# Expert weights stored in blocks of 32 tokens instead of 16, the second block in four lent slots of the row ring

## The reference

```python
x = x + merged @ w_out                       # after pooling, attention and gates
h = rmsnorm(x, g_ffn)
q = (h @ w_query).reshape(C, 8, 2, 128)      # 8 heads, two halves
s = einsum('chpd,hpkd->chpk', q, sub_keys)   # 128 keys per half
sv, si = top_k(s, 16)                        # per half
cand = sv[:, :, 0, :, None] + sv[:, :, 1, None, :]
top_s, pos = top_k(cand, 16)                 # 16 of 256 sums, per head
idx = take_along_axis(cidx, pos)             # expert = 128 * i + j
gate = softmax(top_s)
hid = gelu(einsum('cd,chkd->chk', h, expert_u[idx])) * gate
x = x + einsum('chk,chkd->cd', hid, expert_v[idx])
y = rmsnorm(x, g_final)
```

## Time and profile before

| | us |
|---|---|
| runs | 2788.65, 2793.71, 2780.69; median 2788.65 |
| the profiled execution | 2784.83 |
| its span | 2783.0 |
| PE busy | 2589.6 (93%) |
| DVE busy | 2035.8 (73%) |
| POOL busy | 1556.3 (56%) |
| ACT busy | 537.8 (19%) |
| DMA | 996.18 MB, mean 358 GB/s |
| granted clock of TensorE, mean | 0.972 |

### The profile page before, as it was taken

The page is one execution under the profiler, slowest core; times in us unless marked ns, Lnnn a source line. Parts: engine busy times, 40 slices in busy tenths (PEclk is TensorE's granted clock), DMA queues, the critical chain, the costliest instruction groups (busy, mean ns, idle before and its releaser), DMA issues.

```text
span 2783.0 us, 30841 instructions
## 1 busy us (share of the span) xinstructions
PE 2589.6 (93%) x9957; PEld 1551.2 (56%) x9957; DVE 2035.8 (73%) x4558; ACT 537.8 (19%) x1206; POOL 1556.3 (56%) x1284
## 2 busy tenths in 40 slices
PE   7999989989997998998699999999999999999997
PEld 6867868875334475554554455455545455445553
DVE  1232977877348877788789988977777877877788
ACT  2141151211018014554510000100000000000101
POOL 0000155455665785444277786786777666766674
PEclk9999999989999999999799999999999999999998
DMA  6538789988997898999899999999999999999997
GB/s 239 184 120 299 282 310 406 405 320 312 395 374 254 324 411 319 336 350 333 296 362 413 413 412 413 391 408 413 413 412 413 413 413 413 415 412 413 413 404 285
DMA packets 305988, 996.18 MB, mean 358 GB/s; under 512 B 26432, under 2 KB 107200, under 8 KB 276672
## 3 DMA queue, kind: packets, MB, share of 16 engines
q0 software_dynamic: 184320, 671.17, 62.3%
q1 hardware_dynamic: 69664, 292.02, 26.9%
q10 hardware_dynamic: 51872, 31.46, 3.7%
HBM read 932.68 MB, written 61.87 MB: 357 GB/s over the span
## 4 chain that ended last, share of the span: by engine, by line
PE 34%; DMA 27%; DVE 19%; issue 12%; POOL 3%; ACT 3%; another core or an unknown queue 1%; DVEq 0%; ACTq 0%; POOLq 0%
PE bank L725 13%; DMA ring<-in_expert_v,idx 12%; PE bank L713 9%; DMA ring<-in_expert_u,idx 8%; DVE ring L1464 5%; DMA h<-in_expert_v,idx 3%; PE o_bank L745 3%; POOL ring L1429 2%; PE bank L784 2%; DVE region_b L1481 2%; PE bank L1011 2%; PE o_bank L1001 2%; DMA h<-in_expert_u,idx 1%; DMA region_c<-in_expert_u,idx 1%
## 5 line engine op out<-in xcount | busy, mean ns | idle before, releaser
L1429 POOL DMA_INDIRECT ring<-in_expert_u,idx x465 | 597.9, 1286 | 624.9 <-DVE idx L1772 292.6
L1011 PE MATMUL bank<-wslot,gate_attn 128*128 128x512 f32 x1536 | 690.0, 599 | 26.9 <-DVE gate_attn L1821 26.9
L1001 PE MATMUL o_bank<-region_a,wslot 128*128 128x384 f32 x2048 | 682.4, 487 | 0.0
L1429 POOL DMA_INDIRECT ring<-in_expert_v,idx x423 | 480.9, 1137 | 324.7 <-issue 134.6
L1001 PEld LDWEIGHTS o_bank<-region_a,wslot 128*128 128x128 f32 x2048 | 390.3, 191 | 297.9 <-issue 61.1
L1011 PEld LDWEIGHTS bank<-wslot,gate_attn 128*128 128x128 f32 x1536 | 293.4, 192 | 379.1 <-issue 314.3
L1464 DVE CUSTOM_DVE_ANT_0 ring<-ring,h 128x1024 f32<-128x1024 f32 x377 | 447.3, 1222 | 56.4 <-DMA ring<-in_expert_u,idx 48.6
L1481 DVE SCALAR_TENSOR_TENSOR region_b<-ring,dots,region_b 128x1024 f32<-128x1024 f32 x256 | 328.5, 1283 | 106.0 <-DMA ring<-in_expert_v,idx 78.5
L1331 ACT ACTIVATE gate_attn<-o_bank 128x384 f32<-128x384 f32 x128 | 62.7, 490 | 1241.8 <-PE o_bank L1001 1212.4
L725 PE MATMUL bank<-region_b,wslot 128*128 128x256 f32 (+1 forms) x768 | 232.3, 461 | 1.6 <-ACT region_b L1048 1.6
L725 PE MATMUL bank<-region_a,wslot 128*128 128x256 f32 (+1 forms) x768 | 226.3, 453 | 1.1 <-ACT region_a L1048 1.1
(11 more groups left out here) (214 smaller groups left out, 2860.7 us busy)
## 6 DMA issues: line engine op xcount, KB each, us to landing
wslot<-in_expert_uT SPq DMA_DIRECT2D x64, 1024.0 KB
wslot<-in_expert_v SPq DMA_DIRECT2D x64, 1024.0 KB
wslot<-kept_weights SPq DMA_DIRECT2D x53, 1024.0 KB
kept_weights<-wslot SPq DMA_DIRECT2D x29, 1024.0 KB, 8.6
expert_weights<-region_p ACTq DMA_DIRECT2D x24, 1024.0 KB
wslot<-in_w_in SPq DMA_DIRECT2D x13, 1024.0 KB
region_p<-expert_weights SPq DMA_DIRECT2D x8, 1536.0 KB
region_s<-expert_weights SPq DMA_DIRECT2D x7, 1536.0 KB
```

The lines of the kernel that those rows point to most:

```text
L1001: ins = nc.tensor.matmul(dense_in[q][:, 0:DENSE_T], u_cols[slot][:, k, :], mergeds[1][:, k, T - DENSE_T:T], start=(k == 0), stop=(k == KD ...
L1011: ins = nc.tensor.matmul(dense_out[2 * t + n][:], hidden[q][:, t * P:(t + 1) * P], v_cols[slot][:, n * 512:(n + 1) * 512], start=start, st ...
L1429: nc.gpsimd.indirect_dma_start(ring_row(n), None, expert_u if what == "u" else expert_v, bass.IndirectOffsetOnAxis(ap=ids, axis=0)).then_i ...
```

## The change

A block becomes 32 tokens: eight jobs, 2 MB, 1024 bytes per partition and unit, and 12 stores instead of 24. The DRAM tensor is laid out in 12 blocks per unit. A block now needs 16 KB per partition. The first takes all of what both took in `region_p`. The second lies in slots 0 to 3 of `ring`. For that, `SLOT_OF` leaves these four out for rows 384 to 519, ACT waits before the first job of the second block until the last rows in these slots have been used, and POOL waits before row 520 until the last store of the second block has landed.

```diff
@@ -80,10 +80,15 @@
 ROW = {key: n for n, key in enumerate(ORDER)}
 LATER_SLOTS = (8, 9, 10, 11, 0, 1, 2, 3, 4, 5, 6, 7)
 GUEST, GUEST_ROWS = RING, (SLOTS + RING, 2 * SLOTS + SLOTS // 4)
+LENT, LENT_ROWS = range(4), (3 * SLOTS, 4 * SLOTS + RING - 4)
 SLOT_OF, _next = [n % FIRST_RING for n in range(SLOTS)], collections.deque(LATER_SLOTS)
 for _n in range(SLOTS, len(ORDER)):
     if _n == GUEST_ROWS[0]:
         _next.appendleft(GUEST)
+    if _n == LENT_ROWS[0]:
+        _next = collections.deque(slot for slot in _next if slot not in LENT)
+    if _n == LENT_ROWS[1]:
+        _next.extendleft(reversed(LENT))
     if _n >= GUEST_ROWS[1] and _next[0] == GUEST:
         _next.popleft()
     SLOT_OF.append(_next.popleft())
@@ -96,7 +101,7 @@
 TOKENS_EACH = 4
 W_JOBS = DENSE_T // TOKENS_EACH
 JOBS_PER_TILE = P // TOKENS_EACH
-BLOCK = 16
+BLOCK = 32
 BLOCKS = DENSE_T // BLOCK
 JOBS_PER_BLOCK = BLOCK // TOKENS_EACH
 
@@ -456,7 +461,8 @@
                   for r in sum_places]
         sums = [o[:, :, :].rearrange("p a b -> p (a b)") for o in o_banks]
 
-        blocks = [region_p[:, n * N_KEYS * BLOCK:(n + 1) * N_KEYS * BLOCK] for n in range(2)]
+        blocks = [region_p[:, 0:N_KEYS * BLOCK],
+                  ring[:, LENT.start:LENT.stop, :].rearrange("p a d -> p (a d)")]
         weight_dram = nc.dram_tensor("expert_weights", (P, UNITS, BLOCKS, UNIT_COLS * BLOCK), F32, kind="Internal").ap()
         u_cols = [wslot[:, n // 2, n % 2 * D:(n % 2 + 1) * D].rearrange("p (k i) -> p k i", k=KD)
                   for n in range(COL_SLOTS)]
@@ -1309,6 +1315,9 @@
 
 
                 block = n // JOBS_PER_BLOCK
+                if n == JOBS_PER_BLOCK:
+                    for slot in LENT:
+                        used(act, max(row for row in range(LENT_ROWS[0]) if SLOT_OF[row] == slot))
                 if n % JOBS_PER_BLOCK == 0 and block >= 2:
                     act.wait_ge(block_stored[block % 2], 16 * (block // 2))
                 dst = blocks[block % 2].rearrange("p (u t j) -> p t u j", t=BLOCK, j=UNIT_COLS)
@@ -1421,6 +1430,8 @@
                 if n == SLOTS:
                     filled(pool, LAST_GROUP[0], "h2T", KD - 1)
                     pool.wait_ge(x1_spilled, 16)
+                if n == LENT_ROWS[1]:
+                    pool.wait_ge(block_stored[1], 16 * (BLOCKS // 2))
                 if n == GUEST_ROWS[0]:
                     used(pool, ROW["u", 0, SLOTS - 1])
                 if TURN_OF[n]:
```

## The result

The changed kernel takes 2804.9 us (median of 11 runs, 2797.48 to 2816.18) against 2788.65 us, a ratio of 1.0055 (95% interval 1.0039 to 1.0071): 16 us slower, where 2808 was forecast. Its profiled execution took 2807.4 us (span 2805.6).

A forecast was written before the change was run, and what follows sets the result against it. DMA was taken to pace the column stage, PE just faster; in the query stage PE was nearly always busy. Terms 0 - 3 + 13 + 4 + 10 = +24 on 2784.8 us gave 2809, forecast 2808, range 2790 to 2823.

The forecast's parts named there:

- Longer runs: Stores of expert weights: 17.5 us of DMA time freed, none on the path; counted 0, bounds -17.5 and 0.
- ACT's waits for a store: Last stretch of the weights: ACT's 3.0 us of waits for a buffer go; -3 us, bounds -3 and 0.
- The ring: Query stage: with 8 slots instead of 12, PE's sums wait for gathered rows; +13 us, ends 2 and 21.
- cover: Query stage: PE's 6.3 us of waits for DVE's one-hots absorb some ring delay; half counted, -3 us.
- The clock: Query stage: PE works at a lower granted clock after long waits for rows; +4 us, between 0 and 9.
- Start of the column stage: Four rows gathered later and row 520 waiting for the last store; 5.1 us each, +10.2, ends 5.4 and 13.
- POOL's idle time there goes: Sign expected in the profile after: POOL's idle time in the query stage, 6.04 us before a gather, disappears.
- The short ring is hidden: Rival, query stage: gathers land in about 4.5 to 5 us, ring costs 2; +9, 2794 us; chance 0.24.
- The other side: Rival, query stage: the 17.5 us of freed DMA time come through; -13, 2772 us; chance 0.07.
- Worse on both counts: Rival, query stage: rows land at 8.1 us and each late sum runs at lower clock; +42, 2827 us; chance 0.11.
- the likeliest case: Whole kernel: the forecast itself, 2808 us (2799 to 2818), chance 0.52.

The follow-up runs named there:

- e9: The kernel before (12 slots), each 1 MB store written in runs of 1024 bytes instead of 512, output wrong: ratio to before 0.9991, -1.8 us.
- e10: The kernel before with only the ring shortened to 8 slots, plus 1 MB stores in runs of 1024 bytes, output wrong: ratio to before 1.0131.
- e3: The change, with the four lent slots back in the ring at row 528 instead of 520: ratio to before 1.0134.
- e4: The change with its blocks swapped, so block 0 lies in the lent slots and row 520 waits for the store before last: ratio to before 1.0123.
- e2: The change, with each 2 MB block stored as two 1 MB transfers in runs of 512 bytes, one behind the other: ratio to before 1.0268, +74 us.
- e6: The kernel before with 12 slots, five of the query stage's sum groups moved behind later weights' jobs: ratio to before 1.0070, 18 us slower.

## Why the prediction was right, step by step

**Longer runs, 0.** Right for the kernel before (e9), and incomplete for the change. The fall of ACT's queue from 103 to 87 us was forecast. What I didn't see is that the slack which hides them is taken by the other part of the same change: with 8 slots the same runs are worth some 12 us (e10). It fits that the whole change (1.0135 on the third chip) costs less than its ring alone (1.0162 and 1.0180), but those are other chips, and the change itself moved from 1.0055 to 1.0135 between two. I had listed the two as independent terms and put this gain into a rival by itself.

**ACT's waits for a store, -3.** ACT's waits fell from 3.0 to 1.0 us on the first chip, not to nothing, and from 8.3 to nothing on the third. The rest of the weights, where they stood, is 5.5 us shorter on both chips. In it PE's "issue" waits before its builds fell from 10.1 to 5.5 us on the first chip and from 7.6 to 0.3 on the third; what is behind these is open.

**The ring, +13.** On the first chip 16.3 us of waits against 15.9 worked out, and 5.4 us of cover against 3: +10.9. The mechanism was right and the parts less so, with errors that partly cancel. I took three pairs 7.5 us apart and two of 9.4 to 10.2, each 11.6 us from release to start. All five are 7.6 us apart in the profile after, since PE's waits for the one-hots, which had stretched two of them, are what the delay eats first; and a refill took 10.2 to 11.2 us, so that each wait is about 3.0 us, not 4.1. On the third chip the term is 23.8 with no cover. The Trainium skill (DMA: Bandwidth & Descriptors, Anatomy of one DMA) puts a GpSimd DMA at about 2 us and its bytes at 436 GB/s, 3.2 us for a row as an estimate. By that the full group would stand 7.7 us after the release against 7.6 of distance, and the ring would be hidden. The trace does not agree: 6.1 us from start to landing, with stores, chunks and other rows beside it.

**The clock, +4.** 1.2 us on the first chip, where only one of the waits had a slow group behind it; 7.5 on the third. The bounds 0 to 9 hold both.

**Start of the column stage, +10.2.** The stage is 9.7 us longer, the first product 8.4 us later after the last store (forecast 6.7). The sum was right; its two halves, 5.1 us for the four rows moved behind the start and 5.1 for the transfers missing there, are not separated by any run. What the traces show is that the loss lies ahead of the first product: from there to the end every version takes 1367.2 to 1371.9 us. That price needn't be of the waiting rows: once they don't wait (e3, e4), the 2 MB store and the load behind it are late instead. In the change the store was issued at 1414.76 and the load that waits for it at 1422.55, 7.8 us later. In before this was 8.4 us for 1 MB with gathers beside it; the 8.7 that I took from the earlier trace rows is to the load behind that one. I had it right that the empty engines make up for the size, and e3 and e4 show the other side: 2 MB with gathers beside it took 11.1 and 13.5 us.

**The total.** My terms add up to +24, and the stages measured +16.0: ring +10.9 for 13, clock +1.2 for 4, the rest of the weights -5.5 for -3, start +9.7 for 10.2. That 2808 came within 3.1 us of 2804.9 is partly luck: I counted from the profiled execution, 3.8 us below the median, and from the median the same terms would have given 2813.

**What was to be seen.** PE's waits for rows, six of them; the late first gather into a lent slot; the fewer packets: all there. Only one of the six groups behind the waits was slow on the first chip, and ACT kept 1.0 us of waiting for a store. "POOL's idle time there goes" was wrong: POOL waits 61.3 and 43.2 us for PE's sums in the stage, where before had 64.0 and 26.7, because fewer slots mean that it comes sooner to one that isn't free. Idle time of POOL never was capacity; it was the distance between release and use.

**The rivals.** "The short ring is hidden" fell: landing isn't 4.5 to 5 us. "The other side" fell by e9, and by PE's waits. "Worse on both counts" (+42) is nearly what the third chip shows, +37; my range was made for one chip, and on another chip the likeliest case changed places with a rival.

## What to carry to other kernels

Buffers lent from a ring are paid for at the closest pair of uses: from the timeline take the time from the release to the next use of the slot, with every wait in between removed, since a delay eats those first, and set against it issue plus landing. A saving and a cost in one change aren't two terms to be added if they meet on one resource: longer runs, which were worth nothing with twelve slots, were worth 12 us with eight. The name that a profile gives to the end of a wait is to be checked by counting, when an instruction waits for two things. And where a stage can start only when a store has landed, what is gathered beside that store delays it; early rows are then little gain (2.3 to 2.6 us here).

## What was not expected of the hardware

- Two stores of 1 MB in 2048 runs of 512 bytes, issued by ACT one behind the other, held ACT for 2.5 to 19.5 us (e2), where one took 0.52 us. It takes no pair: in e6 the last of the 24 single stores took ACT 3.98 us, all others 0.52.
- After waits of 3.58 and 3.20 us PE's next group of sixteen matmuls still took 1.92 us on the first chip; after 3.47 and 3.36 us on the third it took 3.64 and 3.33. The length of the wait doesn't settle it on one chip either: after 2.99 us the first chip took 3.14.
- One and the same change cost 0.55% on one chip and 1.35% on another, with both pairs of profiles agreeing on the stages outside the query stage within 1 us.
